# A hybrid decoder layer on one core: gate columns first, projection work between the index matmuls, and a key search with nothing between its rounds

## The reference

```python
z = x @ w_in        # q_a k_a v_a | q_idx k_idx w_idx | q_m k_m v_m o_m | i_m f_m
# group A: 8 heads of 64, sparse attention
logits = einsum('bqhd,bsd->bqhs', q_idx, k_idx) * 32 ** -0.5
score  = einsum('bqh,bqhs->bqs', w_idx * 8 ** -0.5, relu(logits))   # causal, else -1e30
_, idx = top_k(score, 128)          # each query keeps 128 keys, softmax with ALiBi over them
# group B: 4 heads of 128, mLSTM: conv (4 taps) and silu on q_m, k_m; gates i_m, f_m (cumulated),
# decay exp(d_log - m_t), num / den, a normalisation over the head, times sigmoid(o_m)
mix = concat(A, B) @ w_out
# then layer norm, a hierarchical mixture of 32 experts, layer norm, per-layer embedding
```

## Time and profile before

| what | value |
|---|---|
| median of 3 runs | 696.41 us |
| span of the profiled execution | 695.0 us |
| PE busy | 641.7 us (92%) |
| DVE busy | 368.4 us (53%) |
| ACT busy | 178.8 us (26%) |
| POOL busy | 156.4 us (23%) |
| chain that ended last | PE 57%, DVE 9%, DMA 9% |

### The profile page before, as it was taken

How to read it: one execution, slowest core, us unless ns; L and a number is a source line. 1 busy time by engine, 2 the same in 40 slices (tenths; PEclk the granted TensorE clock), 3 DMA queues, 4 the chain that set the end, 5 groups by cost and what they waited for, 6 DMA issues and landing times.

```text
span 695.0 us, 10083 instructions
## 1 busy us (share of the span) xinstructions
PE 641.7 (92%) x3766; PEld 445.1 (64%) x3766; DVE 368.4 (53%) x851; ACT 178.8 (26%) x344; POOL 156.4 (23%) x171
## 2 busy tenths in 40 slices
PE   4999999998999999899957999899999999887997
PEld 4758787776778677788734555555555555543785
DVE  4379999666686648675964223122221112118956
ACT  5165224234322424340211111111111111124321
POOL 4205614000010000041203233233333323211100
PEclk9959999999999999999997999999999999998999
DMA  7402401400400040119986899999999999977003
GB/s 288 155 1 72 171 0 31 181 1 31 151 1 1 1 181 1 37 66 372 384 331 223 294 410 417 417 415 416 412 417 415 414 414 415 406 317 297 21 0 122
DMA packets 30502, 151.21 MB, mean 218 GB/s; under 512 B 7372, under 2 KB 7628, under 8 KB 16496
## 3 DMA queue, kind: packets, MB, share of 16 engines
q1 hardware_dynamic: 24048, 142.08, 51.6%
q0 software_dynamic: 6400, 8.42, 3.4%
HBM read 148.36 MB, written 14.68 MB: 235 GB/s over the span
## 4 chain that ended last, share of the span: by engine, by line
PE 57%; DVE 9%; DMA 9%; issue 3%; SPq 2%; ACT 1%; POOL 1%; DVEq 0%; POOLq 0%; ACTq 0%
PE bank L2021 15%; PE bank L2036 8%; PE bank L1702 8%; PE bank L1704 7%; PE bank L1703 7%; DMA slots<-in_w_exp_dram 4%; PE bank L1782 2%; DMA raw<-in_w_exp_dram 2%; SPq L488 2%; PE bank L2011 2%; PE bank L1791 2%; PE bank L1803 1%; PE bank L1832 1%; PE bank L2028 1%; PE bank L1823 1%
## 5 line engine op out<-in xcount | busy, mean ns | idle before, releaser
L1614 DVE COPY rows_x<-bank 128x128 f32<-128x128 f32 x40 | 11.7, 292 | 189.0 <-PE bank L2028 189.0
L1702 PE MATMUL bank<-w_hi,a_hi 128*128 128x384 f32 (+1 forms) x240 | 89.7, 374 | 3.8 <-POOL w_lo L629 2.8
L1703 PE MATMUL bank<-w_lo,a_hi 128*128 128x384 f32 (+1 forms) x240 | 87.5, 365 | 0.0
L1704 PE MATMUL bank<-w_hi,a_lo 128*128 128x384 f32 (+1 forms) x240 | 87.5, 365 | 0.0
L1702 PE MATMUL bank<-a_hi,w_hi 128*128 128x512 f32 (+1 forms) x176 | 71.2, 404 | 10.2 <-DVE w_lo L1029 8.7
L714 POOL DMA_INDIRECT pair_dram<-rows_x,row_put x40 | 40.5, 1013 | 160.2 <-ACT rows_x L969 160.2
L2021 PE MATMUL bank<-raw,rows_x 128*64 128x256 f32 x640 | 73.7, 383 | 1.1 <-DVE rows_x L1588 0.8
L1703 PE MATMUL bank<-a_lo,w_hi 128*128 128x512 f32 (+1 forms) x176 | 70.0, 398 | 0.0
L1704 PE MATMUL bank<-a_hi,w_lo 128*128 128x512 f32 (+1 forms) x176 | 69.9, 397 | 0.0
L2021 PEld LDWEIGHTS bank<-raw,rows_x 128*64 128x64 f32 x640 | 46.9, 138 | 32.0 <-issue 11.2
L1702 PEld LDWEIGHTS bank<-w_hi,a_hi 128*128 128x128 f32 x240 | 46.1, 192 | 10.5 <-issue 2.5
(11 more groups left out here) (258 smaller groups left out, 1011.3 us busy)
## 6 DMA issues: line engine op xcount, KB each, us to landing
raw<-in_w_exp_dram SPq DMA_DIRECT2D x48, 1024.0 KB, 23.1
slots<-in_w_exp_dram SPq DMA_DIRECT2D x27, 1024.0 KB, 23.2
rows_x<-in_w_exp_dram SPq DMA_DIRECT2D x14, 1024.0 KB, 18.4
raw<-in_w_in_dram SPq DMA_DIRECT2D x19, 512.0 KB, 3.6
y<-in_w_exp_dram SPq DMA_DIRECT2D x7, 1024.0 KB, 22.4
raw<-in_w_wide_dram SPq DMA_DIRECT2D x4, 1536.0 KB, 6.6
raw<-in_w_out_dram SPq DMA_DIRECT2D x4, 1024.0 KB, 5.8
raw<-pair_dram SPq DMA_DIRECT2D x8, 512.0 KB, 6.9
```

Source lines behind the costliest of these rows:

```text
L1702: t_.matmul(o, lh, rh, start=first, stop=False)
L1703: t_.matmul(o, lh, rl, start=False, stop=False)
L1704: return t_.matmul(o, ll, rh, start=False, stop=last)
```

## The change

It moves and resizes the following:

- PE starts with gates_a, then project(0), gates_turn, project(1), project(2), gates_b, index_scores. Between the six sets of index matmuls stand parts of the projections of now = 0 and now = 1 (`BESIDE`).
- DVE runs `gate_rows` and `gate_columns` ahead of `index_sum`; nothing stands between the rounds of `top_keys`. `lstm_add(0)` and the convolutions of head 0 go into the step tables, and the pieces of heads 0 and 1 stand two steps later.
- The low halves of pieces 11 to 13 go from DVE to POOL; the wide pieces 0 and 1 are rounded and halved at other steps (`WIDE_AT`).
- The small gate weights come second in the DMA queue and the first weight piece fifth; the padding of the gate weights is cleared by DVE, not POOL.
- The index and gate halves lie in other places, and the convolution input of head 0 has its own buffer.

```diff
@@ -242,6 +249,12 @@
 
         y_a = y_flat[:, 0:NG * SEQ].rearrange("p (k t) -> p k t", k=NG)
         y_m = y_flat[:, NG * SEQ:].rearrange("p (t c) -> p t c", t=NT)
+        pre_first = y_flat[:, SEQ:SEQ + 2 * 516].rearrange("p (a t) -> p a t", a=2)
+
+        def pre_of(h):
+
+            return pre if h else pre_first
+
         HD = DM // 2
         x_got = [y_flat[:, i * HD:(i + 1) * HD] for i in range(4)]
         xt = [rows_x[:, i * HD:(i + 1) * HD] for i in range(2)]
...
@@ -370,14 +383,18 @@
 
 
         ATTEND = [12, 17, 22, 26]
-        BROADCAST, DECAY_EXP = [5, 15, 20, 28], [8, 16, 21, 29]
-
-        CONV, TANH, CONV_END = [[None, None], [13, 14], [19, 22], [27, 28]], [[9, 10], [15, 15], [22, 23], [28, 29]], [9, 16, 24, 30]
-        HEAD_QK, HEAD_NUM, HEAD_VAR, HEAD_OUT = [12, 17, 24, 30], [14, 19, 26, 32], [15, 20, 26, None], [16, 21, 29, None]
+        BROADCAST, DECAY_ADD, DECAY_EXP = [10, 17, 22, 28], [12, 17, 22, 28], [13, 18, 23, 29]
+
+        CONV, TANH = [[11, 12], [15, 16], [19, 22], [27, 28]], [[12, 13], [17, 17], [22, 23], [28, 29]]
+        CONV_END = [14, 18, 24, 30]
+        HEAD_QK, HEAD_NUM, HEAD_VAR, HEAD_OUT = [14, 19, 24, 30], [16, 21, 26, 32], [17, 22, 26, None], [18, 23, 29, None]
 
         OUT_ROUND, OUT_SPLIT = 29, 30
 
-        POOL_PIECES, POOL_WIDE = 11, 2
+        POOL_PIECES, POOL_WIDE = 14, 2
+
+        WIDE_AT = [1, step_no(1, 0) - 1, step_no(2, 1), step_no(3, 1)]
+        BESIDE = [(0, 0, 3), (0, 3, 6), (0, 6, 8), (1, 0, 2), (1, 2, 4), (1, 4, 8)]
 
         GATE_E = 3
         RT_GROUP, RT_SECOND = 7, 24
...
@@ -447,9 +464,9 @@
             for c in range(4):
                 sp.dma_start(x_raw[:, 2 * c:2 * c + 2, :], d["xT"][:, 2 * c:2 * c + 2, :]).then_inc(s_x[c], 16)
                 if c == 0:
-                    sp.dma_start(raw[:, 0:PW], d["w_in"][0, :, :]).then_inc(s_raw[0], 16)
+                    sp.dma_start(w16[:, :, :], d["w16"]).then_inc(s_w16, 16)
+            sp.dma_start(raw[:, 0:PW], d["w_in"][0, :, :]).then_inc(s_raw[0], 16)
             sp.dma_start(raw[:, PW:2 * PW], d["w_in"][1, :, :]).then_inc(s_raw[1], 16)
-            sp.dma_start(w16[:, :, :], d["w16"]).then_inc(s_w16, 16)
             sp.dma_start(if_bias[:, :], d["if_bias"]).then_inc(s_const, 16)
             sp.dma_start(conv_wb[:, :, :], d["conv_wb"]).then_inc(s_const, 16)
             sp.dma_start(gn_half[:, :], d["gn_w"].partition_broadcast(P)).then_inc(s_const, 16)
...
@@ -654,12 +670,14 @@
             for n in range(NSTEP):
                 grp, j = kind(n)
                 i = piece_at(n)
+                if n == WIDE_AT[1]:
+                    split_wide(1)
+                if i is not None and i + RING < POOL_PIECES:
+                    split(i + RING)
+                if n == WIDE_AT[0]:
+                    split_wide(0)
                 if n == SMALL - 1:
                     strike_future()
-                if i is not None and i + RING < POOL_PIECES:
-                    split(i + RING)
-                if grp is not None and j == 1 and grp < POOL_WIDE:
-                    split_wide(grp)
                 if grp is not None:
                     for h in range(HM):
                         if DECAY_EXP[h] == n - SMALL:
...
@@ -812,6 +830,10 @@
                         act.wait_ge(s_acc, n - 3)
                     a.activation(relu[:, n % 4, 0:(b + 1) * P], index_bank[n % 4][:, 0:(b + 1) * P], ACT.Relu,
                                  scale=DI ** -0.5).then_inc(s_relu, 1)
+                    if n == 15:
+                        evacuate(SMALL)
+                    if n == 19:
+                        round_piece(SMALL + RING)
 
             def softmax(g, u):
                 U, h, b = 8 * g + u, 2 * g + u // NT, u % NT
...
@@ -882,29 +904,30 @@
                 a.activation(a_hi[:, 2 * c:2 * c + 2, :], x_raw[:, 2 * c:2 * c + 2, :], ACT.Copy).then_inc(s_xhi, 1)
 
             round_x(0)
-            round_piece(0)
-            round_x(1)
-            round_x(2)
-            round_x(3)
-            round_piece(1)
             act.wait_ge(s_w16, 16)
             act.wait_ge(s_pad, 2)
             a.activation(w16_hi.rearrange("p k (g c) -> p k g c", g=4)[:, :, :, 0:4],
                          w16.rearrange("p k (g c) -> p k g c", g=4), ACT.Copy).then_inc(s_w16s, 1)
+            round_x(1)
+            round_x(2)
+            round_x(3)
+            round_piece(0)
+            round_piece(1)
             round_piece(2)
+            gates()
             for n in range(NSTEP):
                 grp, j = kind(n)
-                evacuate(n)
+                i = piece_at(n)
+                if n != SMALL:
+                    evacuate(n)
+                    if i is not None and i + RING < NPIECE:
+                        round_piece(i + RING)
+                if n in WIDE_AT:
+                    round_wide(WIDE_AT.index(n))
+                if n == 1:
+                    gates_last()
                 if n == SMALL - 1:
                     index_relu()
-                    gates()
-                i = piece_at(n)
-                if i is not None and i + RING < NPIECE:
-                    round_piece(i + RING)
-                if grp is not None and j == 1:
-                    round_wide(grp)
-                if n == step_no(0, 1):
-                    gates_last()
                 if grp is not None:
                     work(grp, j)
 
...
@@ -1029,17 +1052,20 @@
                 v.tensor_tensor(ring(w_lo, i), raw[:, i * PW:(i + 1) * PW], ring(w_hi, i).bitcast(F32),
                                 ALU.subtract).then_inc(s_wlo, 1)
 
+            v.memset(w16_hi_t[:, :].bitcast(F32), 0.0).then_inc(s_pad, 1)
+            v.memset(w16_lo_t[:, :].bitcast(F32), 0.0).then_inc(s_pad, 1)
             for c in range(4):
                 dve.wait_ge(s_xhi, c + 1)
                 v.tensor_tensor(a_lo[:, 2 * c:2 * c + 2, :], x_raw[:, 2 * c:2 * c + 2, :],
                                 a_hi[:, 2 * c:2 * c + 2, :].bitcast(F32), ALU.subtract).then_inc(s_xlo, 1)
                 if c == 0:
-                    low_piece(0)
+                    dve.wait_ge(s_pad, 2)
+                    dve.wait_ge(s_w16s, 1)
+                    w16_parts = [m.rearrange("p k (g c) -> p k g c", g=4)[:, :, :, 0:4] for m in (w16_lo, w16_hi)]
+                    v.tensor_tensor(w16_parts[0], w16.rearrange("p k (g c) -> p k g c", g=4),
+                                    w16_parts[1].bitcast(F32), ALU.subtract).then_inc(s_w16s, 1)
+            low_piece(0)
             low_piece(1)
-            dve.wait_ge(s_w16s, 1)
-            w16_parts = [m.rearrange("p k (g c) -> p k g c", g=4)[:, :, :, 0:4] for m in (w16_lo, w16_hi)]
-            v.tensor_tensor(w16_parts[0], w16.rearrange("p k (g c) -> p k g c", g=4), w16_parts[1].bitcast(F32),
-                            ALU.subtract).then_inc(s_w16s, 1)
 
             def index_low(n):
                 dve.wait_ge(s_evac, n + 1)
...
@@ -1047,8 +1073,6 @@
                                 ALU.subtract).then_inc(s_ilo, 1)
 
             def gates():
-                index_low(0)
-                index_low(1)
                 dve.wait_ge(s_gate_p, 1)
                 v.tensor_scalar(w_rows, lstm_bank[0][0:WIDX, :], HI_ ** -0.5, None, ALU.mult).then_inc(s_gate_e, 1)
                 dve.wait_ge(s_const, 48)
...
@@ -1119,14 +1142,6 @@
                         dve.wait_ge(s_top, 6 * r + b)
                         v.match_replace(left[:, SO[b]:SO[b] + (b + 1) * P], best[:, b - 1, :], src, TAKEN)\
                             .then_inc(s_top, 1)
-                    if r == 2:
-                        gate_rows()
-                    if r == 7:
-                        gate_columns()
-                    if r == 9:
-                        lstm_add(0)
-                    if r in (11, 13):
-                        convolve(0, (r - 11) // 2)
                 dve.wait_ge(s_top, 6 * (TOPK // 8))
                 for b in range(1, NT):
                     part = left[:, SO[b]:SO[b] + (b + 1) * P]
...
@@ -1319,7 +1336,7 @@
                     if 0 <= now - ATTEND[h] <= 3:
                         normalise(h, now - ATTEND[h])
                 for h in range(HM):
-                    if h and BROADCAST[h] == now:
+                    if DECAY_ADD[h] == now:
                         lstm_add(h)
                     for c in range(2):
                         if CONV[h][c] == now:
...
@@ -1330,6 +1347,11 @@
                     split_out(0)
 
             gates()
+            index_low(0)
+            gate_rows()
+            index_low(1)
+            index_low(2)
+            gate_columns()
             index_sum()
             top_keys()
             for g in range(NG):
...
@@ -1703,20 +1725,19 @@
                 t_.matmul(o, lh, rl, start=False, stop=False)
                 return t_.matmul(o, ll, rh, start=False, stop=last)
 
-            def project(n):
+            def project(n, k0=0, k1=NK):
                 grp, j = kind(n)
                 i = piece_at(n)
```

(29 more changed lines are left out.)

43 lines of the change are left out of this document (27 added, 16 removed).

## The result

| | kernel before | changed kernel |
|---|---|---|
| median, same chip | 696.80 us (4 runs, 696.31 to 697.67) | 689.99 us (4 runs, 687.07 to 698.10) |
| ratio | | 0.987, 95% interval 0.983 to 0.991 |
| profiled execution | span 695.0 us | span 696.3 us (its time: 698.10) |

The profiled execution of the changed kernel is the slowest of its four, and the ratio leaves it out as disturbed; the plain medians give 0.990. Up to half of what sets it apart turns out to be a race in the kernel itself, which the experiments show. In two later sets of runs the unedited kernel gave 0.992 (0.989 to 0.995) both times, by plain medians 0.996 and 0.993. So the change is faster by 0.8 to 1.3%, some 5.5 to 9 us, or by 3 to 7 us if plain medians are compared. The forecast had 1.2 us of gain (695.2 against 696.4), which is too little by any of them.

The account below looks back on a forecast made before the run. PE is busy 166 of 175 us from 118 to 293 us, and PE and DVE's search meet at now = 12. A gain of 9.2 there less 8.0 given back made -1.2 us: 695.2 us, own range 692 to 698, overall 689.0 to 700.0.

Parts of the forecast that it names:

- The front in two cases: Gate rows ahead of the index sums: rows done at 38.0 or 32.4 us, index matmuls starting at 40.0 or 34.4.
- late case: DVE's gn halving and ACT-input operation wait behind POOL's piece 2 until 19.8 us; index matmuls at 40.0, gain 6.5 at now = 12.
- six rows queue behind POOL: At the front, all six DVE row operations take turns with POOL's halvings: 13.4 or 10 us instead of 4.7 alone.
- Projections between the sets: Index start to the end of now = 1: index sets, two projections, slow clock and handovers take 19.8 us.
- Gain at now = 12: PE reaches now = 12 at 111.3 or 106.0 us, not 117.5: gain 6.5 or 11.8, mean 9.2.
- Given back: In the attention steps from now = 12, PE idles 12.8 us more, less 4.8 from shrinking idle times: net loss 8.0 (4 to 12).
- The sum: Whole kernel: mean gain 9.2 at now = 12 less 8.0 lost later gives -1.2 us, 695.2 us; chance 0.45.
- early case: DVE's gn halving and ACT-input operation slip in before POOL's piece 2; index matmuls at 34.4, gain 11.8 at now = 12.
- A shift of the rest, one for one: Behind 293 us nothing is touched, so a gain in the first part shifts the rest by the same amount.
- sign of being wrong: Beyond 345 us, a stretch length changed by more than 1 us would mean the rest is not shifted as a whole.
- Faster: Rival: gate rows meet little POOL work, index matmuls at 33 to 34, PE gains 12 to 15; 690.5 us, chance 0.27.
- Slower: Rival: late front, and stops of 5.8 and 4.7 us at now = 17 and 22 each bring half clock; 700.7 us, chance 0.23.

Follow-up runs that it names:

- early: Changed kernel plus a POOL wait for the third gate row (ACT's input) before halving piece 2; 0.988 of the kernel before, 690.55 us; repeat 0.988, 689.48 us.
- var_conv: Changed kernel with variance and output of head pairs 0 and 1 one step later, pair 2's convolutions at 20 and 21; 0.978, 686.26 us; repeat 0.978, 689.64 us.
- not_beside: Changed kernel with the projections of now = 0 and 1 put whole behind the index matmuls; 1.006 of the kernel before, 702.38 us.
- var_only: Changed kernel with only the variance and output of head pairs 0 and 1 one step later; 0.990 of the kernel before, 691.57 us.
- early_conv: Changed kernel with the added POOL wait, and pair 2's convolutions at 20 and 21 instead of 19 and 22; 0.988 of the kernel before, 689.97 us.
- after_again: The changed kernel run again, unedited; 0.992 of the kernel before, 695.88 us.

## Why the prediction was right or wrong

**The front in two cases: right, and nearly exact.** Forecast: rows done at 38.0 or 32.4, index matmuls at 40.0 or 34.4. Measured: 37.2 and 39.1 in the late case, 31.5 and 34.2 in early. The race of gn's halving, or of the operation behind it (var_conv), with POOL's piece 2 is the one that decides, as the text had it. The step that the six rows queue behind POOL, to which the Trainium skill's lock was put beside (SBUF — State Buffer, "SBUF: two separate sides"), holds: 12.1 us of rows became 4.9 when POOL stayed away. The scans, which the prediction had in doubt, queued too: 3.30 and 2.19 us beside POOL against 1.21 alone.

**Projections between the sets: right.** Forecast 19.8 us from index start to the end of now = 1; measured 19.8 in the changed kernel (39.13 to 58.92) and 19.7 in early. not_beside shows its worth.

**Gain at now = 12: each case mis-sized by about 1.5 us.** Forecast 6.5 and 11.8; measured 8.0 in the late case, 13.1 in early. (The times 111.3 and 106.0 beside these gains are 6.2 and 11.5 from 117.5; the two do not agree by 0.3 us.) The stretch from the end of now = 1 to now = 12 I gave 51.5 us; it took 50.6 in both cases, without a stop of PE. The rest is the front, 0.9 us sooner than forecast in the late case and 0.2 in early.

**Given back: the sum nearly right, its parts less so.** Forecast 8.0; measured 7.2 in the changed kernel and 7.5 in early. At now = 17 I had idle times of 2.3 and 3.5 and found 1.95 and 2.88, at now = 22 4.1 and found 3.40, at now = 12 2.3 and found 1.20. I named the variance first. var_only and early_conv show that the convolution of pair 2 held more of it.

**The sum: wrong, and this is the step that failed.** "Early and late case differ by one race on POOL ... 9.2 is their middle." The gain at now = 12 went into the sum as -9.2, the mean of two cases, and both were too small. None of the six profiles with the changed kernel's own front has the middle: four gain 8.0 to 8.9 us there (after_again among them, with index matmuls at 37.6), two 13.1 and 13.5. (With the added wait it is 10.7 to 13.8, by where the half clock fell.) With the terms as measured it is -0.7 us (late) and -5.5 us (early) at the last wide projection, against +1.5 and -3.8. Three of the four executions in the result took 687 to 691 us, near early's 689 to 692: that fits the early case, though without a profile of them it is not shown. The -6.8 us of the medians would then be early's -5.5 and a part of what the next point adds; how it divides in those executions stays open.

**"A shift of the rest, one for one": wrong.** From the last wide projection to the end of the span it is 409.6 us in the kernel before and 406.5 to 411.6 in the others, with nothing changed there. The first part of it, up to the experts, took 86.0 to 86.6 us in eight profiles and 88.0 to 88.5 in the nine others, kernel before among them; the unedited changed kernel shows both (86.2, 88.5, 86.2). Kernel before, then changed kernel:

```profile
285.44:373.66 88.22, 76.76 (x432) 60.92 (x431) 62.68 (x149) 20.12 (x33) 20.30 (x25) 0.93 0.63 241
```

```profile
284.72:370.95 86.23, 74.55 (x432) 59.45 (x431) 62.64 (x149) 20.11 (x33) 20.23 (x25) 0.96 0.63 245
```

The work is the same and the granted clock is not. Read in slices of 1 us, PE is at half clock for 6.8 to 8.8 us of this stretch in the eight profiles and for 11.7 to 14.1 in the nine. From the experts to the end it is 321.3 us in the kernel before, 325.3 in the changed kernel (10.7 and 17.5 us at half clock) and 321.2 in early (6.8). That is a change of 4 us beyond 345 us, which the prediction had named as a sign of being wrong (over 1 us). So a gain of 5.5 us at 285 us was 7.7 at the experts in early, and the profiled execution of the changed kernel, 2.7 us ahead at the experts, ended 1.3 us behind the kernel before.

**The rivals.** "Faster" gave 690.5 us, near the median, for a reason that was false: rows and POOL did meet. That it came so near is luck. "Slower" needed the late front and stops of 5.8 and 4.7 us. The late front came in two of the three profiles of the unedited kernel and in part in the third, but its stops were 4.8 and 3.4 us. Half clock did not grow with each stop: 3.4, 6.8 and 3.4 us of it stand behind now = 12, 17 and 22, where before had three times 3.4. The range held the median, near its lower end, but by terms and a tail that differ from the forecast's.

## What to carry to other kernels

Where a step can fall to either side of a race, forecast two times and say which one a run takes. Then look for the one wait that fixes it: here a wait on POOL for an operation of 0.7 us was worth 4.3 us against the late front. Taking turns itself cost nothing up to the index matmuls once the order was right. Filling an engine's gaps with work that it has to do anyway paid twice, in time and in clock (9.1 us for two projections). Before a gain is carried over to the end, look at the granted clock of the unchanged part too: here that part varied by up to 5 us between profiles. And when work is moved off a full engine's list, move it as a set: one item alone only moved the stop two steps on.
